# Value products and row release by pair instead of by tile in an expert-retrieval kernel

## The reference

```
act = gelu(einsum("tnd,td->tn", u_tab[eid], xb))      # 128 dots of length 1024 per token
out = einsum("tn,tnd->td", g * act, v_tab[eid])       # weighted sum of 128 value rows
```

## Time and profile before

| | |
|---|---|
| median of 3 runs | 3307.13 us (3300.43 to 3308.66) |
| profiled execution, its own time | 3306.06 us |
| its span in the trace | 3304.0 us |
| mean granted PE clock | 0.794 of full speed |
| mean DMA rate over the span | 375 GB/s |

### The profile page before, as it was taken

The page is one execution under the profiler, slowest core; times in us unless marked ns, Lnnn a source line. Parts: engine busy times, 40 slices in busy tenths (PEclk is TensorE's granted clock), DMA queues, the critical chain, the costliest instruction groups (busy, mean ns, idle before and its releaser), DMA issues. The chain is left out here.

```text
span 3304.0 us, 29348 instructions
## 1 busy us (share of the span) xinstructions
PE 2369.6 (72%) x8956; PEld 944.9 (29%) x8956; DVE 2208.5 (67%) x5442; ACT 991.8 (30%) x2529; POOL 1202.2 (36%) x1072
## 2 busy tenths in 40 slices
PE   7997576888989544886869978746565655676665
PEld 5776142444555100242323534200000000010000
DVE  1525977797457989678755568995767674446554
ACT  1112232332232233334242333323333232323422
POOL 2002343333222344444433343444444443425432
PEclk9998777889989766897989989866666665756666
DMA  8555999899899899999989999999999999989998
GB/s 292 198 186 222 409 406 385 337 356 364 314 370 359 344 346 390 403 419 419 393 356 420 418 420 419 401 377 422 421 421 421 421 422 418 421 344 394 422 423 338
DMA packets 198190, 1239.99 MB, mean 375 GB/s; under 512 B 27952, under 2 KB 27952, under 8 KB 65936
## 3 DMA queue, kind: packets, MB, share of 16 engines
q0 software_dynamic: 149728, 1084.20, 80.5%
q1 hardware_dynamic: 48304, 153.91, 12.3%
HBM read 1229.01 MB, written 9.02 MB: 375 GB/s over the span
## 5 line engine op out<-in xcount | busy, mean ns | idle before, releaser
L1329 POOL DMA_INDIRECT big<-in_experts,eid x710 | 824.9, 1162 | 1551.0 <-PE ps L957 1127.0
L957 PE MATMUL ps<-big,wd 128*32 128x512 f32 x2840 | 807.2, 802 | 518.2 <-ACT wd L1260 508.0
L1966 DVE SCALAR_TENSOR_TENSOR big<-big,xr 128x1024 f32<-128x1024 f32 x710 | 855.0, 1222 | 481.1 <-DMA big<-in_experts,eid 460.7
L1258 ACT ACTIVATE wd<-mask,act 128x32 f32<-128x32 f32 x1024 | 327.8, 320 | 1692.7 <-DVE big L1966 1130.1
L619 PE MATMUL ps<-big,wring 128*128 128x384 f32 (+2 forms) x1584 | 543.6, 494 | 27.9 <-DVE arena L1577 11.1
L957 PEld LDWEIGHTS ps<-big,wd 128*32 128x32 f32 x2840 | 101.9, 122 | 1128.9 <-ACT wd L1260 1035.3
L1329 POOL DMA_INDIRECT more_rows<-in_experts,eid x236 | 267.7, 1134 | 379.0 <-PE ps L957 340.6
L1966 DVE SCALAR_TENSOR_TENSOR more_rows<-more_rows,xr 128x1024 f32<-128x1024 f32 x236 | 284.8, 1223 | 163.2 <-DMA more_rows<-in_experts,eid 159.4
L957 PE MATMUL ps<-more_rows,wd 128*32 128x512 f32 x944 | 268.0, 792 | 171.2 <-ACT wd L1260 169.4
L619 PEld LDWEIGHTS ps<-big,wring 128*128 128x128 f32 x1584 | 300.2, 195 | 286.4 <-issue 91.3
L1260 ACT ACTIVATE wd<-wd,gate 128x32 f32<-128x32 f32 x1024 | 329.0, 321 | 33.1
(11 more groups left out here) (307 smaller groups left out, 2205.3 us busy)
## 6 DMA issues: line engine op xcount, KB each, us to landing
wring<-in_w_in SPq DMA_DIRECT2D x67, 512.0 KB, 8.3
wring<-in_w_q SPq DMA_DIRECT2D x64, 512.0 KB, 8.4
big<-in_experts,eid POOLq DMA_INDIRECT x710, 15.2
wring<-in_w_ada SPq DMA_DIRECT2D x18, 512.0 KB, 4.5
big<-in_w_ada SPq DMA_DIRECT2D x16, 512.0 KB, 7.9
wring<-in_w_out SPq DMA_DIRECT2D x16, 512.0 KB, 8.6
xr<-in_w_ada SPq DMA_DIRECT2D x14, 512.0 KB, 4.2
wring<-in_w_v SPq DMA_DIRECT2D x11, 512.0 KB, 7.8
```

Of the source, the lines that this page charges most:

```text
L957: mm = mmul(ps[QUAD * j:QUAD * (j + 1), half, :], wd[:, 2 * (at % 4) + jj, :], values[:, at_h], start=(m == 0), stop=(m == HALF - 1))
L1258: ac(wd[:, c + jj, :], mask[:], ACT.Gelu, scale=act[:, c + jj:c + jj + 1]).then_inc(S["gelu"], 1)
L1329: gp.indirect_dma_start(row(r), None, t["experts"], bass.IndirectOffsetOnAxis(ap=index, axis=0)).then_inc(s_row[r], 16)
L1966: v.scalar_tensor_tensor(out=row(r)[:, 0:D], in0=row(r)[:, 0:D], scalar=1.0, in1=x, op0=ALU.mult, op1=ALU.mult, accum_out=act[:, c:c + 1]) ...
```

## The change

Both tiles of a pair are multiplied together. PE waits once, for the weights of the second tile, and then issues column half 0 of both tiles and column half 1 of both tiles. `rows_used` rises by 2 after the last product, where it rose by 1 after each tile. Dots, gelus, gates, the number and the shapes of the products, the buffers and the thresholds of all waits on `rows_used` stay.

```diff
-                for jj in range(2):
-                    values = row(PLAN[at][jj][0])[:, D:2 * D]
-                    pe.wait_ge(S["weights"], 2 * at + jj + 1)
-                    for h in range(2):
-                        at_h = slice(512 * h, 512 * (h + 1))
+                values = [row(tile[0])[:, D:2 * D] for tile in PLAN[at]]
+                pe.wait_ge(S["weights"], 2 * at + 2)
+                for h in range(2):
+                    at_h = slice(512 * h, 512 * (h + 1))
+                    for jj in range(2):
                         if b is None:
                             k = 2 * m + jj
-                            mm = mmul(ps[QUAD * h:QUAD * h + NS, 0, :], wmask[:, k, :], values[:, at_h],
+                            mm = mmul(ps[QUAD * h:QUAD * h + NS, 0, :], wmask[:, k, :], values[jj][:, at_h],
                                       start=(k == 0), stop=(k == NS - 1))
                         else:
                             j = 2 * h + jj
-                            mm = mmul(ps[QUAD * j:QUAD * (j + 1), half, :], wd[:, 2 * (at % 4) + jj, :], values[:, at_h],
+                            mm = mmul(ps[QUAD * j:QUAD * (j + 1), half, :], wd[:, 2 * (at % 4) + jj, :], values[jj][:, at_h],
                                       start=(m == 0), stop=(m == HALF - 1))
-                    mm.then_inc(S["rows_used"], 1)
+                mm.then_inc(S["rows_used"], 2)
```

## The result

The changed kernel takes 3312.03 us (median of 20 runs, 3304.43 to 3315.81), the kernel before 3305.84 us over as many (3296.36 to 3309.12). The ratio is 1.0022, with a 95% interval of 1.0015 to 1.0029: slower by some 7 us (5 to 10 by the interval; the medians lie 6.2 us apart), clear of zero and inside the 0.3% that I had called no difference. I had said 3311 us, 5 us slower. The profiled execution is the slowest of the 20; its span of 3313.9 us is 9.9 us longer than that of the trace before, so this one trace shows more than the change's cost.

The account below looks back on a forecast made before the run. The retrieval at the DMA engines' rate (421 GB/s) sets the end, with PE or DVE limiting some stretches. Zero gain on PE plus 5 us for late releases at four dry places: 3306.06 + 5 = 3311.1, taken as 3311 us; range 3300 to 3330.

Parts of the forecast that it names:

- nothing would be gained on PE: Products of a pair ready together already overlap; PE time saved elsewhere lies beside idle time: 0, bounds -7 to 0 us.
- a late release costs nothing in a full queue: From 2300 to 2900 and 3000 on, landing falls from 20.6 to some 18.6 us, far above 5.4: cost 0.
- Place 1: At 1171.90 us, a gather after a pair's first product goes out at about 1173.0 instead: 1.1 us.
- Place 2: Products from 1340.32 to 1343.37 us, soon after which DVE is back at waiting for landings: 1.1 us.
- Place 3: End of the last group's routing, DVE waiting again at 2235.91 us: 1.2 us, the delay of a second gather.
- case (a): Both tiles landed, DVE does dots back to back: first gather 1.12 us late, second at most 1.2 us.
- case (b): DVE waits for each landing: the first tile's gather goes out 2.75 us late, the second's 1.2 us.
- The samples: Sample pairs, queue dry at share 0.84: first release at most 1.7 us later, taken as 1.3 us.
- Rival A: The queue runs dry more often, at more than ten places: 11 to 27 us more, 3317 to 3333; chance 0.12.
- Rival B: From 2300 to 3300 less the samples, every turn of 10 buffers pays 2.75 us: 100 us, 3406; chance 0.02.
- Rival C: From 1300 to 2100 a less busy PE gets a lower clock, slowing the mixer: 19 us, 3330; chance 0.08.
- Rival D: PE's saved time counts from 600 to 1100 and 1300 to 2100: 3299 to 3234 us; chance 0.08.

Follow-up runs that it names:

- double dose: The changed kernel with buffers released only after every second pair, four at once; ratio 1.0197 to the kernel before, 3370.74 against 3304.86 us.
- release only: The kernel before, products still tile by tile, but both row buffers of a pair released together after the second tile's product; ratio 1.0013.
- samples only: The kernel before with the change by pair only in the four sample pairs; ratio 1.0012 (1.0002 to 1.0022).
- PE kept busy: The changed kernel with 12 small zero-weight products added ahead of the weights' wait in pairs 118 to 319; ratio 1.0052 to the kernel before.

## Why the prediction was right

**That nothing would be gained on PE.** Right, by its reason. The overlap was there under the old order, seen in a row of 8 records in 1.06 us. L957's busy time fell by 367 us over the stretches from 300 to 3250 (1163.68 to 796.82), and the kernel is no faster for it.

**That a late release costs nothing in a full queue.** Right from 2300 on; shown by the kernel changed in its last part alone, by the double dose, and by the DMA pieces that shrink from 22 to 16.7 us. For 1300 to 2100 I had put 0 by the share of 0.99 alone, and that reason doesn't hold: the double dose pays 31.8 us from 1457 to 2196. What the single change pays there is lost in the scatter.

**Four places where the queue runs dry, 1.1 + 1.1 + 1.2 + 1.3 us.** Right in kind; place by place the sizes are off. The sum of 5 us was measured as 7 (5 to 10 by the interval). Place 1, taken as 1.1: the trace shows the release 1.2 us late, and six traces pay 0.1 to 1.2 (mean 0.6) where three others gain 0.3 to 0.5. Place 2, taken as 1.1: 1.2 to 2.2 (mean 1.7), with the doubt that a kernel by tile paid 1.3 as well. Place 3, taken as 1.2: 1.2 to 2.6 (mean 1.9). I had priced one delay of case (a) for places 1 and 2 and the delay of a second gather for place 3. Where the pair stands apart by a landing, the first gather is 2.75 us late, my own case (b); that this is what places 2 and 3 pay more is not shown. The samples were taken as 1.3 us, for the first release; the kernel with only them changed says 4, with an interval from 0.7 to 7. The traces put 1.8 to 3.0 us just behind them, and only in the kernels in which one gather takes 6.71 us (last section), which I had not foreseen. That a sum of four such terms came within 2 us is in part luck.

**Rival A**, more dry places: not shown and not closed. With these four places by tile the ratio is 1.0002, whose interval leaves room for 5 us elsewhere, and the stretch from 352 to 608, where the double dose pays most, is the first candidate.

**Rival B**, the loop of latencies: refuted by the double dose, and by 1.0004 for the change in the last part alone, where it expected 1.03.

**Rival C**, the clock: its condition came half true. The clock from 1300 to 2100 fell to 0.85, the limit that I had named, and the mixer's products on `big` and `wring` grew from 494 to 503 ns in the mean over the span. From 1300 to 2100 PE is busy with the mixer for 437 us (612.45 - 175.78) instead of 416, where the rival had 473. The time did not follow: the release alone, at the old clock, costs 1.0013, and the changed kernel with the old clock given back is not faster, though the products that give it back cost time themselves. Between 1.0013 and 1.0023 lies room of 0.001 that the intervals don't close. A microsecond or three may be the clock's.

**Rival D**, faster: refuted. The change makes nothing faster as a whole. Its sign, a shorter stretch from 600 to 1100, shows 1.4 us over 463 us (tiles 96 to 224) in one trace of the changed kernel, and 0.4 us more than before in the other; the kernel with the four places by tile, which costs nothing, has the 1.4 us too.

## What to carry over

Before a product is packed more tightly, look in the trace at two that are ready together: if they already overlap, the packing can only delay what the early one released. A release that comes later is free as long as the queue that it feeds is deep, so ask where it is deep and where it runs dry, and don't take a DMA share of 0.99 for depth: the stretch with 0.99 paid half of the double dose, the one with 1.01 none of it. And a chain of waits made of long transfers is no loop of latencies when the shortest such transfer takes a quarter of the median.

## What the runs showed of the hardware

A gather on POOL, 0.94 us when undisturbed, can take 6.71 us. The timeline of the changed kernel after the sample pairs:
```profile
2982.55 6.71 POOL L1329 DMA_INDIRECT big<-in_experts,eid  x1 [0.30 <-issue]
2982.66 1.20 DVE L1966 SCALAR_TENSOR_TENSOR more_rows<-more_rows,xr 128x1024 f32<-128x1024 f32 x1
...
2987.24 1.21 DVE L1966 SCALAR_TENSOR_TENSOR big<-big,xr 128x1024 f32<-128x1024 f32 x1
...
2989.56 0.94 POOL L1329 DMA_INDIRECT big<-in_experts,eid  x1 [0.30 <-issue]
```
and of the kernel before at the same place:
```profile
2973.49 1.86 POOL L1329 DMA_INDIRECT big<-in_experts,eid  x1 [0.43 <-PE ps L953]
...
2978.10 4.28 POOL L1329 DMA_INDIRECT big<-in_experts,eid  x1 [2.75 <-PE ps L957]
...
2980.35 1.21 DVE L1966 SCALAR_TENSOR_TENSOR big<-big,xr 128x1024 f32<-128x1024 f32 x1
```
DVE does five dots without a pause from 2982.66 to 2988.45, and the gather ends at 2989.26, 0.81 us after the last. It is the gather that takes the buffer of the last sample tile. In the kernel before that gather (2973.49) is sent 2.28 us ahead of DVE's run, which starts at 2975.77, and takes 1.86 us; it is the next one, sent 2.33 us into the run, that takes 4.28 us, and it ends at 2982.38, 0.82 us after the run (2981.56). In all five traces whose sample pairs are released together (the changed kernel twice, release only, samples only, PE kept busy) this gather goes out 0.11 us ahead of the run and takes 6.71 us. With samples released by tile it takes 1.5 to 2.0 in eight traces, and the next one 4.27 to 4.34 in six of them and 5.42 and 5.49 in the two with the products later in PE's order. In the double dose, where the releases stand otherwise, no gather there takes more than 3.3. The price shows at the dot that needs the long gather: it waits 5.91 us, where it waited 0.96 before:
```profile
2994.36 1.23 DVE L1966 SCALAR_TENSOR_TENSOR big<-big,xr 128x1024 f32<-128x1024 f32 x1 [5.91 <-DMA big<-in_experts,eid]
```
Of POOL's 31 us more of busy time the two gathers make 1.5 (4.85 more and 3.34 less). Gathers that take more than 1 us are 439 of 1032 instead of 402; that these too are such meetings is not shown. The Trainium skill ("SBUF — State Buffer", "SBUF: two separate sides") says that DVE and GpSimd share a port pair as an exclusive lock, taken also by a DVE operation with two SBUF inputs against a GpSimd operation that reads SBUF, and that the loser blocks. The trace agrees in that the gather ends only after the run of dots does; no run here took the dots away to test it. These five traces are also the ones that pay 1.8 to 3.0 us just after the samples, where seven others, the double dose aside, pay 0.0 to 1.3. So the longer gather, at a place where the queue is dry, is likely the part of the samples' cost that I had not priced; no run separates it from the late first release.

The granted clock answers to small products with zero weights: 12 of them for a pair, 8 columns wide, brought the clock from 0.85 back to 0.91 from 1300 to 2100, and from 0.53 to 0.65 from 1100 to 1300.
